# A two-block layer on one core: the second mixer joined with its tail, the GLU's products placed among the attention's pairs

## The reference, cut to what matters

```python
h = rms(x, norm1) * (1 + sc1) + sh1
u, q, k, v = split(h @ w_in)                      # 512, 512, 128, 128 columns
# state-space part
y = scan(u) @ c + d_skip * u
z = gelu(y)
y_ssm = z * sigmoid(z @ w_glu + b_glu)            # the GLU, 512 x 512
# attention: 8 query heads, 2 key heads, window 128, a sink per head
y_attn = softmax(q k^T / 8 + bias, with sink) @ v
mixed = concat(rms(y_ssm, o_ssm), rms(y_attn, o_attn))
x = x + g1 * (mixed @ w_out)
h2 = rms(x, norm2) * (1 + sc2) + sh2
x = x + g2 * conv_ffn(h2)
```

## Time and profile before

| | us |
|---|---|
| median of 3 runs | 1252.51 (1252.3 to 1253.71) |
| the profiled execution | 1248.42 |
| its span | 1246.3 |
| border, last feed-forward product to first input product | 673.9 to 680.5 |
| input products | 680.5 to 752 |
| attention | 753 to 810.3 |
| tail up to the output projection | 810.3 to 826.2 |
| output projection and r6 | 826.2 to 876.7 |

### The profile page before, as it was taken

One profiled execution on the slowest core, in us unless ns is written; L12 is line 12 of the kernel. 1 busy time (PEld: TensorE's weight loads), 2 busy tenths in 40 slices (PEclk: granted clock), 3 DMA queues, 4 the chain that ended last, 5 costly groups with the idle time before them and its releaser, 6 DMA issues. The chain is left out here.

```text
span 1246.3 us, 14741 instructions
## 1 busy us (share of the span) xinstructions
PE 1201.6 (96%) x5909; PEld 938.9 (75%) x5909; DVE 772.5 (62%) x1274; ACT 486.8 (39%) x744; POOL 62.1 (5%) x76
## 2 busy tenths in 40 slices
PE   7999998899999999999998999789899999999998
PEld 5786666468778788878886885578688888888887
DVE  6537574756677777775876587656765543455542
ACT  6244545725322212222375234673444421343320
POOL 0000000013100000000022000034000000000000
PEclk9999999999999999999999999999999999999999
DMA  9312121223465576353226531102122223332222
GB/s 355 130 64 68 35 68 34 102 81 128 148 228 193 172 248 248 127 177 116 76 96 170 179 109 35 35 34 102 58 82 97 80 94 114 102 101 101 70 93 91
DMA packets 31884, 144.67 MB, mean 116 GB/s; under 512 B 3303, under 2 KB 9672, under 8 KB 22600
## 3 DMA queue, kind: packets, MB, share of 16 engines
q1 hardware_dynamic: 31816, 143.73, 33.9%
HBM read 136.90 MB, written 6.82 MB: 115 GB/s over the span
## 5 line engine op out<-in xcount | busy, mean ns | idle before, releaser
L133 PE MATMUL bank<-xhi_ffn,w_hi_part 128*128 128x512 f32 x704 | 278.2, 395 | 4.4 <-DVE xlo_ffn L233 4.4
L121 ACT ACTIVATE w_hi_part<-w_raw 128x2048 fp32r<-128x2048 f32 (+1 forms) x95 | 164.1, 1727 | 289.1 <-PE bank L135 287.3
L134 PE MATMUL bank<-xlo_ffn,w_hi_part 128*128 128x512 f32 x704 | 275.7, 392 | 0.0
L135 PE MATMUL bank<-xhi_ffn,w_lo_part 128*128 128x512 f32 x704 | 274.9, 391 | 0.0
L127 DVE TENSOR_TENSOR w_lo_part<-w_raw,w_hi_part 128x2048 fp32r<-128x2048 f32 (+1 forms) x95 | 195.4, 2057 | 94.5 <-ACT w_hi_part L121 91.3
L133 PEld LDWEIGHTS bank<-xhi_ffn,w_hi_part 128*128 128x128 f32 x704 | 132.6, 188 | 35.0 <-issue 6.6
L135 PEld LDWEIGHTS bank<-xhi_ffn,w_lo_part 128*128 128x128 f32 x704 | 132.6, 188 | 30.4
L134 PEld LDWEIGHTS bank<-xlo_ffn,w_hi_part 128*128 128x128 f32 x704 | 132.4, 188 | 28.5 <-issue 0.2
L361 DVE SCALAR_TENSOR_TENSOR squares<-bank,param,squares 128x511 f32<-128x511 f32 x88 | 63.9, 747 | 84.7 <-ACT squares L344 83.1
L133 PE MATMUL bank<-hhi,w_hi_part 128*128 128x512 f32 x240 | 94.6, 394 | 0.3 <-DVE w_lo_part L127 0.3
L133 PE MATMUL bank<-hhi_half,w_hi_part 128*128 128x512 f32 x240 | 94.1, 392 | 0.0
(11 more groups left out here) (359 smaller groups left out, 1789.8 us busy)
## 6 DMA issues: line engine op xcount, KB each, us to landing
mod_w<-in_w_mod SPq DMA_DIRECT2D x32, 768.0 KB, 4.4
w_raw<-in_w_gu SPq DMA_DIRECT2D x22, 1024.0 KB, 6.4
w_raw<-in_w_down SPq DMA_DIRECT2D x32, 704.0 KB, 4.2
w_raw<-in_w_up SPq DMA_DIRECT2D x22, 1024.0 KB, 4.9
w_raw<-in_w_in_f SPq DMA_DIRECT2D x8, 1024.0 KB, 4.9
w_raw<-in_w_out SPq DMA_DIRECT2D x8, 1024.0 KB, 4.9
w_raw<-in_w_in SPq DMA_DIRECT2D x5, 1024.0 KB, 4.9
x<-in_x SPq DMA_DIRECT2D x8, 256.0 KB, 6.0
```

The costliest lines, as they stand in the source:

```text
L121: act.activation(k.whi[:, slot, 0:width], k.raw[:, slot, 0:width], ACT.Copy).then_inc(k.w_hi, 1)
L133: pe.matmul(out, whi, xhi, start=first, stop=False)
L134: pe.matmul(out, whi, xlo, start=False, stop=False)
L135: return pe.matmul(out, wlo, xhi, start=False, stop=last)
```

## The change

- **Border.** The eight transposes go ahead of `r3.pe_sum`, into banks 2 and 3; `r3` sums in bank 0; `lag_weights` follows it, still ahead of the input products. DVE, no longer ACT, copies the transposed blocks. POOL's zeroing of the lag tile waits for the first `inputs`.
- **Attention.** The state-space pieces move to earlier pairs. At pair 9 ACT loads the Gelu table, does four Gelus and loads the table of exp and tanh. At pairs 10 and 11 ACT rounds and DVE rests the four z tiles. At pairs 12 to 15 PE makes the GLU, 12 products a pair, all in bank 6: each waits for the tanh of the one before. Sigmoid becomes 0.5 (1 + tanh(x/2)), the halves put in constants. Roundings, rests and squares of the outputs stand among the last pairs.
- **Tail.** It stays in the same block: no barrier. The state-space half is projected first. `r4` and `r5` add three squares on POOL and give the fourth to PE, so each `pe_sum` has one matrix product more. `w_used` for the GLU chunk is counted after PE's wait for its own last product.

DVE and then PE at the border:

```diff
+            for a in range(2):
+                dve.wait_ge(bt_made, a + 1)
+                dve.tensor_copy(bt[:, a, :], k.bank[2 + a][:, :]).then_inc(bt_sb, 1)
+            border_rest(dve, 0, border_hi, 1, border_lo)
...
+            pe.wait_ge(angled, 4)
+            for a in range(2):
+                for t in range(4):
+                    mm = pe.transpose(k.bank[2 + a][:, P * t:P * t + P], powers[:, 0, a, t, :], k.ident)
+                mm.then_inc(bt_made, 1)
+            r3.pe_sum(pe, k, KT - 2, [KT - 1])
+            lag_weights()
```

The pieces' places, then ACT's new functions and its loop over the pairs:

```diff
-        LAGS_AT, STATES_AT, OUTPUT_AT = (2, 5, 8), (3, 6, 10), (1, 4, 7, 11)
-        SPIN_AT = (1, 3, 5, 7, 9)
+        LAGS_AT, STATES_AT, OUTPUT_AT = (2, 4, 6), (3, 5, 7), (1, 4, 6, 8)
+        SPIN_AT = (0, 1, 2, 3, 4)
+        GELU_AT, GLU_AT = 9, 12
...
+            def attn_round(g):
+                act.wait_ge(l_stored, g + 1)
+                plain_round(act, r5, ahi[:, g, :], y[:, 4 + g, :], o_attn[:, g:g + 1])
+                r5.act_square(act, k, y[:, 4 + g, :], g)
+            def gate_tanh(t):
+                act.wait_ge(sm_made, t + 1)
+                act.activation(tanhs[:, t, :], k.bank[6][:, :], ACT.Tanh, bias=b_half[:, t:t + 1], scale=0.5)\
+                    .then_inc(sm_sig, 1)
+            def ssm_round(t):
+                act.wait_ge(sm_done, t + 1)
+                plain_round(act, r4, shi[:, t, :], y[:, t, :], o_half[:, t:t + 1])
...
-                if p == 6:
+                if p == 7:
                     next_weights(OUT2)
                 if p >= NT + 2 and p % NT == 2:
                     store(p // NT - 1)
+                if p == GELU_AT:
+                    act.preload_act_table_set("gelu_apprx_tanh_and_others")
+                    for t in range(4):
+                        act.wait_ge(y_sum, t + 1)
+                        act.activation(y[:, t, :], y[:, t, :], ACT.Gelu_apprx_tanh).then_inc(sm_gelu, 1)
+                    act.preload_act_table_set("exp_and_others")
+                if p in (GELU_AT + 1, GELU_AT + 2):
+                    for t in (0, 1) if p == GELU_AT + 1 else (2, 3):
+                        act.wait_ge(sm_gelu, t + 1)
+                        act.activation(zhi[:, t, :], y[:, t, :], ACT.Copy).then_inc(sm_zhi, 1)
+                if p == GELU_AT + 3:
+                    attn_round(0)
+                    attn_round(1)
+                if p == PAIRS - 1:
+                    attn_round(2)
+                if p > GLU_AT:
+                    gate_tanh(p - GLU_AT - 1)
+                if p > GLU_AT + 1:
+                    ssm_round(p - GLU_AT - 2)
+            ssm_round(3)
+            r4.act_square(act, k, y[:, 0, :], 0, 0.5)
+            r4.act_square(act, k, y[:, 1, :], 1, 0.5)
             store(3)
+            attn_round(3)
+            r4.act_square(act, k, y[:, 2, :], 2, 0.5)
+            r4.act_square(act, k, y[:, 3, :], 3, 0.5)
```

DVE's functions and loop:

```diff
+            def split_z(t):
+                dve.wait_ge(sm_zhi, t + 1)
+                dve.tensor_tensor(zlo[:, t, :], y[:, t, :], zhi[:, t, :].bitcast(F), ALU.subtract).then_inc(sm_zlo, 1)
...
+            def gate(t):
+                dve.wait_ge(sm_sig, t + 1)
+                dve.scalar_tensor_tensor(out=y[:, t, :], in0=tanhs[:, t, :], scalar=1.0, in1=y[:, t, :], op0=ALU.add,
+                                         op1=ALU.mult).then_inc(sm_done, 1)
...
-                if p == 2:
+                if p == 6:
                     next_rest(GLU)
                 if p == 8:
                     next_rest(OUT2)
+                if p in (GELU_AT + 1, GELU_AT + 2):
+                    for t in (0, 1) if p == GELU_AT + 1 else (2, 3):
+                        split_z(t)
+                if p == GELU_AT + 3:
+                    attn_rest(0)
+                    attn_rest(1)
+                if p == PAIRS - 1:
+                    attn_rest(2)
+                if p > GLU_AT:
+                    gate(p - GLU_AT - 1)
+                if p > GLU_AT + 1:
+                    ssm_rest(p - GLU_AT - 2)
+            gate(3)
+            ssm_rest(2)
+            ssm_rest(3)
+            attn_rest(3)
```

PE's GLU:

```diff
+            def glu(t):
+                if t == 0:
+                    pe.wait_ge(k.w_lo, GLU + 1)
+                    pe.wait_ge(sm_zlo, 4)
+                else:
+                    pe.wait_ge(sm_sig, t)
...
+                for j in range(4):
+                    mm = split_mm(pe, k.bank[6][:, :], hi[:, j, P * t:P * t + P], lo[:, j, P * t:P * t + P],
+                                  zhi[:, j, :], zlo[:, j, :], j == 0, j == 3)
+                mm.then_inc(sm_made, 1)
+                if t == 3:
+                    pe.wait_ge(sm_made, 4)
+                    pe.sem_inc(k.w_used, 1)
...
+                if p >= GLU_AT:
+                    glu(p - GLU_AT)
                 if p == 1:
                     pe.wait_ge(h2_root, 2)
                 turn(p)
             values(NT - 1)
```

The tail, PE and ACT:

```diff
+            from_s(0)
+            r4.pe_sum(pe, k, 2, [3])
+            from_a(0)
+            r5.pe_sum(pe, k, 2, [3])
+            pe.wait_ge(l_stored, 4)
+            from_s(1)
+            pe.wait_ge(part_s, 2)
+            from_a(1)
...
+            round_chunk(act, k, (OUT2 + 1) % 2, 16 * ((OUT2 + 1) // 2 + 1), OUT2)
+            act.preload_act_table_set("natural_log_exp_and_others")
+            r4.act_root(act, 4, eps_col[:, 0:1])
+            r5.act_root(act, 4, eps_col[:, 0:1])
```

More of the change, by code:

```diff
@@ L196, in pe_sum @@
             pe.wait_ge(self.squared, j + 1)
-            mm = pe.matmul(self.bank[:, :], k.ones[:, :], k.sq[:, j % 4, :], start=False, stop=j == tail[-1])
+            mm = pe.matmul(self.bank[:, :], k.ones[:, :], self.sq[:, j % 4, :], start=False, stop=j == tail[-1])
         mm.then_inc(self.summed, 1)
@@ L2122, in _ @@
             pool.wait_ge(hot_in, 32)
+            pool.wait_ge(v_made, 1)
+            pool.wait_ge(lag_sum, 1)
             nc.clear_and_free_semaphores(feed_sems)
+            pool.memset(lag[:, :, :, :], 0.0).then_inc(lag_zero, 1)
+        r5 = Norm(k, "r5", square_sum, root_attn, k.bank[7])
+        r4 = Norm(k, "r4", sum_b, root_ssm, k.bank[6], ssm_squares)
+        sm_gelu, sm_zhi, sm_zlo, sm_made, sm_sig, sm_done = (
+            k.sem(f"glu_{w}") for w in ("gelu", "z_rounded", "z_split", "made", "tanh", "done"))
         @block.scalar
@@ L2185, in _ @@
             act.activation(rel_rows[:, :], k.bank[3][:, 0:384], ACT.Copy).then_inc(rel_sb, 1)
-            for a in range(2):
-                act.wait_ge(bt_made, a + 1)
-                act.activation(bt[:, a, :], k.bank[4 + a][:, :], ACT.Copy).then_inc(bt_sb, 1)
             first_tile(IN2 + 1, 2, k.bank[0])
@@ L2435, in lag_weights @@
             def lag_weights():
+                pe.wait_ge(bt_sb, 2)
                 for i in range(16):
@@ new lines, in program, with _ @@
+        ffn2 = FeedForward(k, "ffn2", UP2, io["w_up2"], io["w_down2"], xhi6, xlo6, hhi6, hlo6)
+        bank_s, bank_a = (4, 2, 0, 4), (0, 4, 2, 0)
+        @block.sync
+        def _(sp):
+            for n in range(OUT2 + 3, ffn2.last):
+                load_chunk(sp, k, n % 2, io["w_out2"][n - OUT2] if n < UP2 else ffn2.source(n), after_lo=n - 1)
+            for j in range(KT):
+                sp.wait_ge(ffn2.added, KT + j + 1)
+                sp.dma_start(io["out"][:, j, :], x[:, j, :]).then_inc(stored, 16)
+            sp.wait_ge(stored, 16 * KT)
@@ new lines, in _, with add_ssm @@
+        @block.gpsimd
+        def _(pool):
+            def add_ssm(j):
+                pool.wait_ge(part_s, j + 1)
+                pool.tensor_tensor(x[:, j, :], x[:, j, :], part[:, j % 2, :], ALU.add).then_inc(added_s, 1)
+            for j in (1, 2):
+                r5.add(pool, k, j)
+            r4.add(pool, k, 1)
+            r4.add(pool, k, 2)
+            for j in range(4):
+                add_ssm(j)
+            r6.add(pool, k, 1)
+            for j in (4, 5):
+                add_ssm(j)
+            r6.add(pool, k, 2)
+            r6.add(pool, k, 3)
+            for j in (6, 7):
+                add_ssm(j)
@@ L2792, in program @@
-        gone(tail_ctx)
         gone(mid_ctx)
```

359 lines of the change are left out of this document (138 added, 221 removed).

## The result

The changed kernel takes 1257.79 us (median of 7 runs, 1255.05 to 1260.14) beside 1252.9 for the kernel before on the same chip. The ratio is 1.0034, with an interval of 1.0024 to 1.0045: 4.3 us slower. Measured once more, it was 1.0038 (1.0025 to 1.0051). The prediction said 1254.5, in a range of 1246.5 to 1259.5.

A forecast was written before the change was run, and what follows sets the result against it. PE was taken to bound the kernel, at work 1201.6 of 1246.3 us. Border -4.5, attention +4.8 and tail +1.7 made +2.0: 1250.4 us profiled, 1254.5 against the median, range 1246.5 to 1259.5.

The forecast's parts named there:

- Border, -4.5 forecast: At the border: work moved out of busy stretches -2.81, wait for the last square +0.1, clock held -1.8; in all -4.5 us.
- The moved work, forecast at 2.7: Border: transposes (0.85 us) and lag weights (1.96) leave stretches where PE never waits, -2.81, with +0.1 at the last square.
- I take it that the clock holds: Border: PE's clock stays up behind a new pause of about 1.9 us, -1.8 us, bounds 0 and -1.8.
- Rival 2: Border: the clock falls all the same behind the 1.9 us pause, +1.8 us, 1256.3 us; chance 0.15.
- a like pause at 215 us: Evidence for the border's clock: elsewhere, behind a pause of about 2 us, PE's next stretch still ran at 1.00.
- Attention up to pair 12, +6.3 forecast: Attention: table loads, Gelus, roundings and moved pieces make pair 12's exponentials 6.3 us later, at 804.2.
- the upper bound of 8.7: Attention up to pair 12: upper bound of the delay, given as 6.8 + 1.9 us; lower bound 3.0.
- The waits for ACT's `output` inside its own pair: Attention: `lags(2)` and `lags(3)` stand in the pair whose `output` on ACT they wait for; only `scores` fill that wait.
- The ring, 21.9 forecast: Pairs 12 to 15: each GLU group waits for the previous tanh; rounds 4.7, 5.2, 5.8, last part 6.2, sum 21.9 us.
- the 2.0 charged for cold products: Attention: `values(2)` and the first GLU group run cold after the Gelu lull, +2.0 us, bounds 0 and 3.8.
- Third rival, a drain at each table switch: ACT amid the pairs: two drains as long as the table load add 2.6 us, 1257.1 us; chance 0.03.
- Tail, +1.7 forecast: Tail: each `pe_sum` gets a second matrix product of 0.86 us, +1.7 us; late squares up to 1 us.

The follow-up runs named there:

- the second experiment: The changed kernel with ACT's tanh of a GLU group ahead of the move of the same pair: ratio 1.0012 to the kernel before, 3.0 us faster than the changed kernel.

## Why the prediction came out as it did

The time, 1257.8, lies 3.3 us above the one forecast. The direction, a little slower because the rest of the change takes back more than the border gives, was right, with most of the mechanism. The sizes all erred one way, and that the time came so near is in part luck, as the last point says.

- **Border, -4.5 forecast, -2.5 in the trace.** The moved work, forecast at 2.7, is gained: the border part alone gives 2.6 by its trace and 3.1 by the timed runs. The step that failed is "I take it that the clock holds". Rival 2 was true of six of the seven profiles with that pause, this one among them. The row it leaned on, a like pause at 215 us behind which the clock held, was one outcome of two: behind the same wait of 2.11 us in the same code the block took 2.4 us in nine of the thirteen profiles and 3.7 to 4.1, at clock 0.58 to 0.62, in the other four, the changed kernel's own among them.
- **Attention up to pair 12, +6.3 forecast, +8.8 and +9.3 measured**, both over the upper bound of 8.7 and the largest miss of the sum. The block itself is as forecast: loads 1.28, four Gelus 2.19, no gap. What the queues were followed without is DVE's first moved piece in pair 0, where DVE isn't yet ahead: PE waited 3.47 us in pair 1 in place of 1.54. Putting the pieces one pair later gave back 1.9 us of that wait, and 2.0 us in the timed runs. The waits for ACT's `output` inside its own pair were forecast in kind, and one cost 1.34.
- **The ring, 21.9 forecast.** From 811.27 to 834.65 it is 23.4. The intervals were right within 0.4 us; the 1.5 over are the last part (7.90 in place of 6.2), with the fourth group partly at the low clock. The first group came 4.15 us after pair 12's exponentials, where 2.9 and the 2.0 charged for cold products make 4.9; so C missed by only 0.7. The cause named, the tanh behind the move, is what the second experiment confirms.
- **Third rival, a drain at each table switch.** ACT's next instruction starts 0.02 us behind the end of the load (800.33 + 1.28, then 801.63), and PE's wait shrank by 1.42 with one load gone, not by 2.6. So the drain that the Trainium skill ("ScalarE: Activation LUTs", What ACT_TABLE_LOAD costs) adds doesn't show in this chain either.
- **Tail, +1.7 forecast, +3.0 measured.** From the projection's first product to the sum for the last norm it is 45.62 to 45.64 us in the three kernels with the old tail, 47.01 to 47.04 with one second product and 47.85 to 47.88 with two. So a second product costs 0.85 us, as priced, and 0.5 us more lie within the projection, whose cause stays open. The rest, 0.7, lies behind that sum, in code that the change doesn't touch: there the thirteen profiles have anything from 374.5 (the one of before) to 376.4, and the second feed-forward's first 10 us, behind a wait of 4.35 us in all of them, ran at a clock of 0.70 to 0.83.
- **The sum.** The four misses are 2.0, 2.5, 0.7 and 1.3: +8.5 in place of +2.0. That the time missed by only 3.3 is luck, owed to the offset between profile and median. I added 4.1 us to both kernels alike; but the profile of before, 1248.42, lies 4.5 under the median measured beside the changed kernel, and that of after, 1259.53, lies 1.7 over its own. Part of that offset can be seen. The kernel with the border part alone has the same code as before from the attention on, and its profile lost 2.9 us there against that of before: 1.6 in C, at clock 0.77 in place of 0.88, and 1.3 in D, where the second feed-forward's first 10 us ran at 0.72 in place of 0.83. So it is the clock behind waits, which comes out one way or the other. What decides it stays open.

## What to carry to other kernels

Filling a pause of the busiest engine with work from elsewhere paid here at its full length; the clock behind it is a second prize, won in one of seven profiles with a pause left and in all five without one, and two needless products were enough for that. Before work is put amid a stretch that three engines pass through in turn, ask for each what stands behind it in the same queue: one tanh behind a move and DVE's pieces a pair too early made up 5 of the 7.6 us that this change lost. And before a forecast leans on one row for what the clock does behind a pause, look for the same row in a second profile of the same code. Where an engine is fed in its last moment, a product more on it can be cheaper than an addition on another that contends with a third.

## What the runs showed of the hardware

The same instructions behind the same 1.90 us wait ran at the full clock in one profile (11.26 us) and partly at the lower one in six (12.9 us). Elsewhere, behind a wait of 2.11 us in code that no edit touches, the block took 2.4 us at clock 1.00 in nine profiles and 3.7 to 4.1 at 0.58 to 0.62 in four. The time of the kernel before went with its mean granted clock from one execution to the next: 1248.2 to 1250.3 us at 0.992 to 0.993, 1252.0 to 1254.8 at 0.985 to 0.989. A whole execution ran at a mean clock of 0.555 once, on one core: 2034.5 us, with the same kernel at 1255.5 to 1258.3 in the eleven others. An addition on POOL and a rest on DVE that meet stretch each other from 2.6 to 4.5 (two additions) and from 2.3 to 3.4 us.
